# Last layer norm of a two-layer trunk, finished token tile by token tile instead of both tiles together

## The reference

```python
def layer_norm(x, g, b):
    mu = jnp.mean(xf, axis=-1, keepdims=True)
    var = jnp.mean(jnp.square(xf - mu), axis=-1, keepdims=True)
    return ((xf - mu) * lax.rsqrt(var + LN_EPS)) * g + b
...
        y = conv_ffn(u, w_up[l], conv_w[l], conv_b[l], w_down[l])
        x = layer_norm(ALPHA * x + (1.0 + g2) * y, ln_g[l, 1], ln_b[l, 1])
    return x
```

## Time and profile before

| | us |
|---|---|
| median of the 3 runs | 2278.12 |
| the profiled execution, its own time | 2276.89 |
| its span in the trace | 2275.1 |
| TensorE busy | 2233.1 (98%) |
| VectorE busy | 1694.9 |
| ScalarE busy | 1009.4 |

### The profile page before, as it was taken

How to read it: one execution, slowest core, us unless ns; L and a number is a source line. 1 busy time by engine, 2 the same in 40 slices (tenths; PEclk the granted TensorE clock), 3 DMA queues, 4 the chain that set the end, 5 groups by cost and what they waited for, 6 DMA issues and landing times.

```text
span 2275.1 us, 27917 instructions
## 1 busy us (share of the span) xinstructions
PE 2233.1 (98%) x11205; PEld 1856.6 (82%) x11205; DVE 1694.9 (74%) x1671; ACT 1009.4 (44%) x1011; POOL 8.4 (0%) x19
## 2 busy tenths in 40 slices
PE   7999999999999999999999999999999999999999
PEld 3777777888888888888788888878888788888886
DVE  2789999768878878788877767684688756565565
ACT  2445344454433444443355444434544334444432
POOL 1000000000000000000000000000000000000000
PEclk9999999999999999999999999999999999999999
DMA  9999899868889978889787777865687756665652
GB/s 369 386 409 352 304 320 347 291 220 277 288 283 344 307 270 289 270 277 325 293 308 256 279 254 253 303 215 167 215 281 279 260 190 205 190 194 186 223 190 105
DMA packets 392227, 612.66 MB, mean 269 GB/s; under 512 B 21113, under 2 KB 205073, under 8 KB 390562
## 3 DMA queue, kind: packets, MB, share of 16 engines
q1 hardware_dynamic: 387314, 608.29, 76.4%
q10 hardware_dynamic: 4336, 2.33, 0.3%
q0 software_dynamic: 448, 0.25, 0.0%
HBM read 608.70 MB, written 2.10 MB: 268 GB/s over the span
## 4 chain that ended last, share of the span: by engine, by line
PE 56%; DVE 2%; issue 1%; ACT 0%; DMA 0%; DVEq 0%; ACTq 0%
PE banks L1444 32%; PE banks L1576 14%; PE banks L1584 7%; DVE w_lo L940 1%; DMA ada_w<-in_w_ada 0%; PE banks L1507 0%; PE banks L1920 0%; PE banks L1887 0%; PE banks L1908 0%; PE banks L1679 0%; PE banks L1897 0%; PE banks L1957 0%; PE banks L1952 0%; DVE ada_acc L956 0%; ACT w_hi L598 0%
## 5 line engine op out<-in xcount | busy, mean ns | idle before, releaser
L940 DVE TENSOR_TENSOR w_lo<-w_raw,w_hi 128x2048 fp32r<-128x2048 f32 x380 | 847.8, 2233 | 384.5 <-ACT w_hi L598 332.3
L598 ACT ACTIVATE w_hi<-w_raw 128x2048 fp32r<-128x2048 f32 x380 | 710.2, 1870 | 826.3 <-PE banks L1444 498.2
L1576 PE MATMUL banks<-u_hl,w_hi 128*128 128x512 f32 x2368 | 574.4, 392 | 0.0
L1576 PEld LDWEIGHTS banks<-u_hl,w_hi 128*128 128x128 f32 x2368 | 433.3, 188 | 85.6 <-issue 2.3
L1444 PE MATMUL banks<-w_hi,u_hl 128*128 128x512 f32 x1920 | 480.6, 403 | 10.7 <-ACT u_hl L663 4.1
L1444 PEld LDWEIGHTS banks<-w_hi,u_hl 128*128 128x128 f32 x1920 | 363.9, 193 | 95.7 <-issue 16.5
L1584 PEld LDWEIGHTS banks<-u_hl,w_lo 128*128 128x128 f32 x2368 | 308.4, 191 | 15.5 <-DVE w_lo L940 1.2
L1584 PE MATMUL banks<-u_hl,w_lo 128*128 128x256 f32 x2368 | 313.3, 283 | 0.3 <-DVE w_lo L940 0.3
L1444 PE MATMUL banks<-w_hi,hid_hi 128*128 128x512 f32 x688 | 270.1, 393 | 0.0
L1444 PE MATMUL banks<-w_hi,hid_lo 128*128 128x512 f32 x688 | 267.9, 389 | 0.0
L956 DVE SCALAR_TENSOR_TENSOR ada_acc<-ada_w,silu_c,ada_acc 128x1024 f32<-128x1024 f32 x187 | 239.3, 1280 | 15.4 <-DMA ada_w<-in_w_ada 9.2
(11 more groups left out here) (229 smaller groups left out, 1244.9 us busy)
## 6 DMA issues: line engine op xcount, KB each, us to landing
ada_w<-in_w_ada SPq DMA_DIRECT2D x352, 512.0 KB, 6.6
w_raw<-in_w_up SPq DMA_DIRECT2D x344, 512.0 KB, 4.7
w_raw<-in_w_down SPq DMA_DIRECT2D x152, 512.0 KB, 4.9
w_raw<-in_w_qkv SPq DMA_DIRECT2D x96, 512.0 KB, 4.8
w_raw<-in_w_in_ab SPq DMA_DIRECT2D x64, 512.0 KB, 9.1
ada_w_more<-in_w_ada SPq DMA_DIRECT2D x32, 512.0 KB, 10.8
w_raw<-in_w_out_ab SPq DMA_DIRECT2D x32, 512.0 KB, 6.4
w_raw<-in_w_o SPq DMA_DIRECT2D x32, 512.0 KB, 4.9
```

Source lines behind the costliest of these rows:

```text
L598: nc.scalar.activation(whi[:, u % HL_SLOTS, 0:width], raw[:, u % RAW_SLOTS, 0:width], ACT.Copy).then_inc(w_hi, 1)
L940: nc.vector.tensor_tensor(wlo[:, u % HL_SLOTS, 0:width], raw[:, u % RAW_SLOTS, 0:width], whi[:, u % HL_SLOTS, 0:width].bitcast(f32), ALU.s ...
L1576: ins = nc.tensor.matmul(bank[banks[s] + i][:, :], tile(whi, k, s, i), uhl[:, kt].rearrange("p a s -> p (a s)"), start=first and k == 0, s ...
```

## The change

The last norm goes tile by tile. Tile 0's statistics, root and t are computed as soon as tile 0 is complete, between the instructions of tile 1. The shift t*g + b is one product of two rows with two rows: `tail_rows` holds t as a row and a row of ones (2 x 128), `tail_gb` holds g and b (2 x 2048, loaded by two transfers of 8 KB ahead of `down_b`). To get t as a row, TensorE multiplies the column t with the identity (a product 1 x 128), and ScalarE copies it out. For the pieces (tile 0, chunk 0) and (0, 1), TensorE also adds x times a diagonal matrix of rs, so the bank holds the finished output and ScalarE copies it to `x`; the other six are ended by VectorE. The products with b by the identity, which ran right behind `down_b`, are gone. The output leaves in eight transfers of 256 KB.

```diff
-TAIL_ORDER = (3, 0, 1, 2)
+TAIL_ACT = [(0, 0), (0, 1)]
+TAIL_DVE = [(0, 3), (0, 2), (1, 3), (1, 0), (1, 1), (1, 2)]
+TAIL_OUT = [(0, 0), (0, 3), (0, 2), (0, 1), (1, 3), (1, 0), (1, 1), (1, 2)]
...
                     ln_load(3)
+                    for k, name in enumerate(("ln_g", "ln_b")):
+                        sp.dma_start(tail_gb[k:k + 1, :], A[name][1, 1:2, :]).then_inc(sem("tail_in"), 16)
...
+            tail_sd(0)
+            tail_row(0)
+            tail_sd(1)
+            tail_copy(0)
+            tail_row(1)
+            tail_copy(1)
...
+                dve.wait_ge(y_done, 23)
+                dve.wait_ge(y_half, 4)
+                link(product(0))
+                link(added(0))
+                variance(0)
+                nc.vector.memset(tail_rows[:, :, :], 1.0).then_inc(sem("tail_ones"), 1)
+                dve.wait_ge(w_used, unit_no((1, "down_b"), c, PH[1, "down_b"]["n"]))
+                link(product(1))
+                root(0)
+                nc.vector.tensor_scalar(tail_diag[:, :], ident, rs[:, 0:1], None, ALU.mult).then_inc(sem("tail_diag"), 1)
+                link(added(1))
+                variance(1)
+                link(centred(0))
+                root(1)
+                ended(0)
+                ended(1)
+                link(centred(1))
+                for i in range(2, len(TAIL_DVE)):
+                    ended(i)
...
-            pe.wait_ge(sem("ln_in"), 32 * 4)
+            def tail_row(t):
+                pe.wait_ge(sem("tail_t"), t + 1)
+                nc.tensor.matmul(bank[2 + t][0:1, 0:P], t1[:, t:t + 1], ident, start=True, stop=True
+                                 ).then_inc(sem("tail_row"), 1)
+
+            def tail_shift(t, n, stop=True):
+                return nc.tensor.matmul(bank[TAIL_BANKS[n] + t][:, :], tail_rows[:, t, :],
+                                        tail_gb[:, n * NCOL:(n + 1) * NCOL], start=True, stop=stop)
+
+            def tail_whole(n):
+                tail_shift(0, n, False)
+                nc.tensor.matmul(bank[TAIL_BANKS[n]][:, :], tail_diag[:, :], x[:, 0, n * NCOL:(n + 1) * NCOL],
+                                 start=False, stop=True).then_inc(sem("tail_full"), 1)
+
+            tail_row(0)
+            pe.wait_ge(sem("tail_in"), 32)
+            pe.wait_ge(sem("tail_row_out"), 1)
+            pe.wait_ge(sem("tail_diag"), 1)
+            tail_whole(0)
+            tail_shift(0, 2).then_inc(sem("tail_shift"), 1)
+            tail_row(1)
+            tail_whole(1)
+            pe.wait_ge(sem("tail_row_out"), 2)
             for n in range(3):
-                for t in range(NT):
-                    nc.tensor.matmul(bank[TAIL_BANKS[n] + t][:, :], ident, lnp[:, 1, n * NCOL:(n + 1) * NCOL],
-                                     start=True, stop=False)
...
+                tail_shift(1, n).then_inc(sem("tail_shift"), 1)
```

More of the change, by code:

```diff
@@ L230, in build @@
         wlo = place("w_lo", [P, HL_SLOTS, UNIT], region(HL_SLOTS * UNIT * 4), f32r)
-        ada_w = place("ada_w", [P, ADA_SLOTS, 2 * NCOL], region(ADA_SLOTS * 2 * NCOL * 4))
+        r_ada = region(ADA_SLOTS * 2 * NCOL * 4)
+        ada_w = place("ada_w", [P, ADA_SLOTS, 2 * NCOL], r_ada)
         ada_acc = place("ada_acc", [P, 2 * NCOL], region(2 * NCOL * 4))
@@ L289, in build @@
         acc_alt = place("ada_acc_alt", [P, 2 * NCOL], r_s + 4096)
-        tail_diag = place("tail_diag", [P, NT, P], r_s)
+        tail_rows = place("tail_rows", [2, NT, P], r_s)
+        tail_diag = place("tail_diag", [P, P], r_s + NT * P * 4)
+        tail_gb = place("tail_gb", [2, D], r_ada)
         att_hi = place("att_hi", [P, NT, 3 * D], r_w, f32r)
@@ L922, in _, with tail_sd, tail_copy @@
             mlp(1)
-            ln_sd(3)
+            def tail_sd(t):
+                act.wait_ge(sem("tail_var"), t + 1)
+                nc.scalar.activation(sd[:, t:t + 1], var[:, t:t + 1], ACT.Sqrt).then_inc(sem("tail_sd"), 1)
+            def tail_row(t):
+                act.wait_ge(sem("tail_ones"), 1)
+                act.wait_ge(sem("tail_row"), t + 1)
+                nc.scalar.activation(tail_rows[0:1, t, :], bank[2 + t][0:1, 0:P], ACT.Copy
+                                     ).then_inc(sem("tail_row_out"), 1)
+            def tail_copy(i):
+                t, n = TAIL_ACT[i]
+                act.wait_ge(sem("tail_full"), i + 1)
+                nc.scalar.activation(x[:, t, n * NCOL:(n + 1) * NCOL], bank[TAIL_BANKS[n] + t][:, :], ACT.Copy
+                                     ).then_inc(sem("tail_act"), 1)
+            tail_sd(0)
[4 more added lines that the diff above has]
+            tail_copy(1)
         @block.vector
@@ L1043, in tail @@
                     cs = slice(c * NCOL, (c + 1) * NCOL)
+                    if (key, c) == ((1, "down_b"), 3):
+                        return
                     if (key, c) in Y_LAST:
@@ L1090, in rstd, with layer_norm @@
                 link(nc.vector.tensor_tensor(r, r, t, ALU.mult))
-            def layer_norm(s, last, after=None):
-                dve.wait_ge(y_done, {0: 4, 1: 12, 2: 16, 3: 24}[s])
+            def layer_norm(s, after):
+                dve.wait_ge(y_done, {0: 4, 1: 12, 2: 16}[s])
                 for t in range(NT):
@@ L1097, in layer_norm @@
                 nc.vector.tensor_scalar(var, mv[:, :, 1], EPS, None, ALU.add).then_inc(sem("ln_var"), 1)
-                if not last:
-                    ln_quarters(s, 0, 4 if s == 1 else 2)
+                ln_quarters(s, 0, 4 if s == 1 else 2)
                 dve.wait_ge(sem("ln_var"), s + 1)
                 rstd(var, sd, rs, t1, "ln_var", "ln_sd", s + 1)
-                if last:
-                    link(nc.vector.scalar_tensor_tensor(t1, mv[:, :, 0], -1.0, rs, ALU.mult, ALU.mult))
-                    for t in range(NT):
[L1105 to L1123, removed]
                 half = NCOL // 2
@@ L1133, in layer_norm, with last_norm, product, added @@
                 lo_unit(after)
+            def last_norm():
+                c = 3
+                cs = slice(c * NCOL, D)
+                b = DOWN_BANKS["down_b"][c]
+                def product(t):
+                    return nc.vector.tensor_tensor(y_tmp[:, t, :], bank[b + t][:, :], gate[:, cs], ALU.mult)
+                def added(t):
+                    return nc.vector.scalar_tensor_tensor(x[:, t, cs], x[:, t, cs], 1.0, y_tmp[:, t, :],
+                                                          ALU.mult, ALU.add)
+                def variance(t):
+                    link(nc.vector.bn_stats(bn[:, t, c, :], x[:, t, cs]))
+                    link(nc.vector.bn_aggr(mv[:, t, :], bn[:, t].rearrange("p c s -> p (c s)")))
+                    nc.vector.tensor_scalar(var[:, t:t + 1], mv[:, t, 1:2], EPS, None, ALU.add
+                                            ).then_inc(sem("tail_var"), 1)
+                def root(t):
+                    v, sdv, r, to = (a[:, t:t + 1] for a in (var, sd, rs, t1))
+                    dve.wait_ge(sem("tail_sd"), t + 1)
+                    link(nc.vector.reciprocal(r, sdv))
+                    link(nc.vector.scalar_tensor_tensor(to, r, r, v, ALU.mult, ALU.mult))
+                    link(nc.vector.tensor_scalar(to, to, -0.5, 1.5, ALU.mult, ALU.add))
+                    link(nc.vector.tensor_tensor(r, r, to, ALU.mult))
+                    nc.vector.scalar_tensor_tensor(to, mv[:, t, 0:1], -1.0, r, ALU.mult, ALU.mult
+                                                   ).then_inc(sem("tail_t"), 1)
+                def centred(t):
+                    return nc.vector.scalar_tensor_tensor(x[:, t, cs], x[:, t, cs], mv[:, t, 0:1], lnp[:, 0, cs],
+                                                          ALU.subtract, ALU.mult)
+                def ended(i):
+                    t, n = TAIL_DVE[i]
+                    at = slice(n * NCOL, (n + 1) * NCOL)
+                    if n < 3:
+                        dve.wait_ge(sem("tail_shift"), [t_n for t_n in TAIL_DVE if t_n[1] < 3].index((t, n)) + 1)
+                    shift = lnp[:, 1, at] if n == 3 else bank[TAIL_BANKS[n] + t][:, :]
+                    nc.vector.scalar_tensor_tensor(x[:, t, at], x[:, t, at], rs[:, t:t + 1], shift, ALU.mult, ALU.add
+                                                   ).then_inc(sem("tail_dve"), 1)
+                dve.wait_ge(y_done, 23)
[17 more added lines that the diff above has]
+                    ended(i)
@@ L1404, in _ @@
                 beside(ATT_U + u)
-            layer_norm(2, False, unit_no((1, "up_a"), 0, 1))
+            layer_norm(2, unit_no((1, "up_a"), 0, 1))
             mlp(1)
-            layer_norm(3, True)
+            last_norm()
         @block.gpsimd
@@ L1948, in _, with tail_row @@
             pe.wait_ge(acc_free, evacuated((1, "down_b"), 2) + 1)
-            pe.wait_ge(sem("ln_in"), 32 * 4)
-            for n in range(3):
-                for t in range(NT):
-                    nc.tensor.matmul(bank[TAIL_BANKS[n] + t][:, :], ident, lnp[:, 1, n * NCOL:(n + 1) * NCOL],
```

(6 more changed lines are left out.)

15 lines of the change are left out of this document (9 added, 6 removed).

## The result

The changed kernel takes 2284.39 us in the median of 11 runs (2281.83 to 2289.22), the kernel before 2277.34 in 11 runs beside it (2270.33 to 2282.11). The ratio is 1.0035, 95% interval 1.0026 to 1.0044: slower by about 7 to 8 us, where no change was forecast, with 2278.8 and a range up to 2281.2. What came true is in the main the rival with the least chance of its own (0.03), a clock at half to the end.

A forecast was written before the change was run, and what follows sets the result against it. TensorE was taken to set the tail's end: +1.2 us for the later last piece, -0.5 for the smaller last transfer, so +0.7 on 2276.89, plus 1.23 to the runs' median: 2278.8 us, range 2276.2 to 2281.2.

The forecast's parts named there:

- The rival of half clock to the end: TensorE stays at half clock from 2263.65 to the end of its work: +4.8 us, 2282.9; chance 0.03.
- What bounds the tail: From VectorE's first product of tile 0 (2258.22) to the span's end: TensorE, not VectorE, sets the changed kernel's end.
- the end at full clock: VectorE's last piece ends at 2271.91 if TensorE's clock stays full, 0.05 us earlier than before.
- The price of a product with two rows: Tail's shift products on TensorE: 0.86 us each, as with 128 rows; half of it as lower bound.
- I therefore take the clock to fall shortly before or after 2263.65, and to cost the smaller of the two, 1.5, as TensorE then has an unbroken list.: Behind `down_b`, idle time drops TensorE's clock to half for a while, costing 1.5 us; chance of this short loss 0.45.
- The places on which I had based the 1.5 and 2.5: After the norms near 1130 and 1530 us, idle times and short products precede units taking 5.34 and 6.28, undisturbed 3.79.
- the 0.23 that an idle moment takes up: Part of the clock loss falls into TensorE's idle moment before tile 1's row product, so 0.23 us is subtracted.
- rows 10: Profile rows on TensorE after the norms near 1130 and 1530 us, giving losses of 1.5 and 2.5 us.
- The rule of the Trainium skill: It warns only of idle gaps longer than the one behind `down_b`; by it the clock stays full.
- the row that I set against it: The idle gap of 2.22 us near 1130, taken as enough to drop TensorE's clock.
- Transfers: Last output transfer shrinks from 512 to 256 KB, saving 0.5 us (0 to 0.65); the two 8 KB loads cost nothing.
- The spread between runs: Runs of one kernel were taken to differ by 1.4 us (2278.08 to 2279.51), which entered the range's upper end.

The follow-up runs named there:

- experiment 4: Changed kernel with its two-row shift products zero-padded to 128 rows and the gap behind `down_b` filled by three 128-row products: 2275.47 us, ratio 0.9997 to the kernel before.
- experiment 3: Changed kernel with the gap behind `down_b` filled by three products of two rows: 2285.19 us, ratio 1.0040 to the kernel before.
- experiment 2: Changed kernel with the gap behind `down_b` filled by three products of 128 rows, two-row products kept: 2282.94 us, ratio 1.0027 to the kernel before.
- experiment 5: Kernel before the change, with its six products with b using one row instead of 128: 2281.67 us against 2276.71, ratio 1.0019.
- experiment 1: Changed kernel with its two-row shift products zero-padded to 128 rows, gap behind `down_b` kept: 2277.55 us, ratio 1.0007 to the kernel before.
- experiment 6: The version of experiment 4 with four output transfers of 512 KB instead of eight of 256 KB: 2276.91 us, ratio 0.9998 to the kernel before.

## Why the prediction was wrong

**What bounds the tail:** right. Both lists, VectorE's and TensorE's, hold to two tenths: t of tile 0 was forecast 4.4 behind VectorE's first product and came at 4.5; TensorE's first large product 5.43 behind it, and it came at 5.46; the end at full clock 13.69, and experiment 4 has 13.88. That TensorE and not VectorE would set the end is seen there too, by the 0.47 of idle time with TensorE as releaser.

**The price of a product with two rows:** right as duration, between products of equal rows. It is the columns that cost: the passes of experiment 3's filling follow each other 0.43 apart, so 0.86 for two, and 0.86 was taken. Next to a product of 128 rows it was too low: 1.02 at full clock and 2.0 at half, which no row of before could show. And it was wrong to look at the duration alone.

**"I therefore take the clock to fall shortly before or after 2263.65, and to cost the smaller of the two, 1.5, as TensorE then has an unbroken list."** This is the step that failed: the end of the fall and so its cost, 1.5, where the clock stayed down to the last product and the tail lost 6.8 against experiment 4. The fall itself came, at about 2266. The reason given for its end did not hold, because most of the large products from there on (the shift (0, 2), the first half of piece (0, 1), the three shifts of tile 1) have two rows and only one, the product with x of piece (0, 1), has 128, and experiments 2, 3 and 5 show that such products do not hold the clock; in the changed kernel and in experiment 2 a list made up mostly of them did not bring it back either. The places on which I had based the 1.5 and 2.5 are followed by products with 128 rows. With 128 rows in the tail, experiment 1, the gap costs 1.7 where 1.3 was forecast (1.5 less the 0.23 that an idle moment takes up): for the kernel that I thought I had before me, the number was near. That is in part luck, for the two losses of rows 10 are not fixed to their places: the ten traces have the same work there, and the unit behind the norm near 1130 takes 5.21 to 6.65 us in them, the one near 1530 5.24 to 6.47. An experiment's 1.7, read from one execution, can be off by as much; over all runs the ratios of experiments 1 and 4 differ by 0.0010, 2.3 us.

**The rival of half clock to the end** had nearly the size (2282.9, measured 2284.4), but a chance of 0.03, and it named no reason for which the clock should stay down; that the time lies near its price is in part luck. It has the half clock from 2263.65 on, and it began later. Its price was too small: I scaled the passes by 16 to 9, counting passes that overlap the ends of a stretch. VectorE's last pieces above start 1.71 apart, which is a product of two passes at half clock, against 0.86: a factor of 2.0, not 1.8. From the first large product to the end of the last it is 14.4 us, where 12.6 were forecast, although the first 1.7 us still ran at full clock; about 1 us of it are the changes between two and 128 rows.

**The rule of the Trainium skill** that was weighed against the trace, on idle gaps ("TensorE: Matmul & The Clock Gate", "Why this matters for your kernels"), was not contradicted by the row that I set against it. Near 1130 the granted clock was 1.00 through the idle 2.22 us and through the eight short products behind them, and fell only in the second idle stretch, the 1.22 of the earlier trace rows (1.00 over 1131.20 to 1132.50, 0.86 over 1132.50 to 1133.70, 0.50 behind): from the start of the first to the end of the second it is 4.7 us, with TensorE busy for 1.3 of them. In experiment 1 it is 3.5 us from the end of `down_b` (2258.59) to the first large product (2262.14), with a short product of 0.38 in it. So each of these places is longer than its first gap, and neither decides between the rule and my row. What experiments 1 and 4 show is that the stretch as a whole costs 1.7. But both the rule and my row spoke of gaps, and the larger part of the loss needs none: 5.8 us in experiment 2, where the gap is filled, and 3.7 in experiment 5.

**Transfers:** right. The landing of 256 KB takes 2.1 us (median), against 2.7 for 512 KB; 0.5 was taken and 0.6 measured. That the smaller transfers matter more in the order by tiles than in the old one, the prediction did not see; experiment 6 puts it at 1.6. The two loads of 8 KB cost nothing: SyncE issues them within 0.6 us, in a stretch in which it had nothing else to issue, and the next load of weights follows 1.35 later.

**The spread between runs** was underrated. The three runs shown lay within 1.4 us; 11 of the same kernel span 12. The interval of the ratio, not a single profile, carries the verdict.

## What to carry to other kernels

Replacing a product over all 128 rows by one over a few rows of the same columns saved nothing in its own duration here (0.86 us either way, and more next to a product of 128 rows), and it can take the clock of everything behind it. Where the padding is free, as with zero rows here, pad to 128 (only one and two rows were tried against 128). When work is reordered so that TensorE's first instruction waits for a result of another engine, ask what keeps it at full clock meanwhile, and look at rows of the operands as well as at busy time. Output that is finished by tiles should also leave by tiles: big transfers that need the last tile all become ready close together.

## What the runs showed of the hardware that I had not expected

- A TensorE that the profile shows as 100% busy can lose its full clock. With one row (experiment 5), passes without a pause from 2260.07 were enough; the granted clock was 1.00 until 2264.6 and 0.51 from 2264.8.
- At half clock it does not recover on a mixture: in the changed kernel, one large product of 128 rows among five of two rows left it at 0.50 for over 12 us.
- Rows that hold only zeros on both sides count like others: experiment 1 came back from 0.51 to 1.00 under one product with 126 of 128 rows zero and one with x (2262.14 to 2265.6), and stayed at 1.00 over the rest, where five of six large products have 126 zero rows (the shift (0, 2) among them) and one is with x.
- A float32 product of 512 columns takes 0.86 us at 2.4 GHz and about 1.7 at 1.2 GHz among products of equal rows: with two rows 1.71 (VectorE's last pieces in the changed kernel), with 128 rows 1.73 and 1.71 (experiment 1, starts at 2262.14, 2263.87 and 2265.58). A product with two rows next to one with 128 takes 2.0 at half clock (L2029 and L2034 of the changed kernel); the next load of weights then starts with its product and not ahead of it.
